# Two joined transformer blocks on one core: other tail of the expert stage, other places for a softplus exponential, weight loads, a copy, a z product, weight differences and a gate tile

## The chip, the cores and the metric

One core of one Trainium2 chip runs the whole program. The metric is the device time of one execution in microseconds (us); all arithmetic is float32. The engines are TensorE (PE, with its weight loads as PEld), VectorE (DVE), ScalarE (ACT), GpSimd (POOL) and SyncE (SP, which here issues most transfers). They run their own instruction lists and wait for each other on semaphores.

## The reference, cut to what matters

The input has 256 tokens of width 1024. The first block is attention over a low-rank key/value, a gated MLP over chunks, and a mixture of 32 experts; the second is two layers, each an RG-LRU branch and an mLSTM branch.

```python
h = rms_norm(x, norm1_g); proj = h @ w_in            # q, ckv, qi, ki, wi, u, v, ga, gb
merged = sigmoid(ga) * (attention @ w_proj_a) + sigmoid(gb) * (gmlp(u, v) @ w_proj_b)
x = x + merged @ w_out
h2 = rms_norm(x, norm2_g)
comb = two experts of one group per token            # router
y = sum over e of comb[:, e] * ((silu(h2 @ w_gate[e]) * (h2 @ w_up[e])) @ w_down[e])
x = rms_norm(x + y, final_norm_g)
for l in range(2):
    shift, scale, gate = split(silu(c) @ w_ada[l] + b_ada[l])
    h = rms_norm(x, norm_g[l]) * (1 + scale) + shift
    rg_x, rg_z, ml_x, ml_o, ml_z = split(h @ w_in[l])
    y_rg = rglru(conv(rg_x), softplus(-lambda)) * silu(rg_z)
    y_ml = norm(sigmoid(ml_o) * mlstm(silu(conv(ml_x)))) * silu(ml_z)
    x = x + gate * (concat(y_rg, y_ml) @ w_out[l])
return rms_norm(x, final_g)
```

## The kernel before, in words

**Weights and slots.** SP issues every big weight as one 1 MB piece (load, L1177 to L1183): 49 first pieces (24 of them slices of w_ada), 96 expert chunks (gate, up, down of 32 experts) and 64 layer pieces. A piece goes to a slot and SP waits until the piece that lay there before is used up. The first and the layer pieces share a ring of 6 slots; the expert chunks use 19 slots, the ring and 13 other buffers that are idle in that stage (L440 to L450). Nine expert chunks are issued between first pieces, behind the pieces of EARLY_LOADS (L87). SP works strictly in order, so a wait for one slot holds all that stand behind it.

**First block.** PE multiplies piece after piece. The order of the first pieces is: two of qi, ada 0, the latent piece, ada 1, two of q, u 0, ada 2, u 1, ada 3, v 0, ada 4, ada 5, v 1, ada 6, ada 7, then gate pieces alternating with ada pieces. An ada piece is not for PE: DVE sums it (ada_sums, L1620), or, for six of them, POOL multiplies it (L2326) and ACT sums the product (ada_job, L1257), ADA_LAG places later than the call asks for. Until that is done its ring slot is taken. After the index scores ACT waits for sp_wanted (L1309), a DVE step (L1659 to L1662), for the exponential of a softplus that only the layers need; behind it on ACT stand the copies of K and V out of PSUM (L1311 to L1314), without which PE has no free bank for V (L588). Then come u, v, two gate jobs (L623) and the loop over 8 heads (L625), in which PE turns the probabilities of head g once DVE has them ready (L635).

**Expert stage.** The router's counts decide an order of the experts; only the six fixed experts (18 chunks) can be asked for before it is known (L1218 to L1221). Nine units (gate_up_own, turn, down_own, gather, mix; L790 to L841) take two or four experts each, every expert in its own 32 or 64 columns of the array. mix(u) adds the result of a unit to the tokens: 4 matmuls on PE, 4 additions on DVE (L1880). After the last unit DVE adds and takes statistics (L1930 to L1948), POOL multiplies by final_norm_g (L2350), ACT squares (L1438), and from both sums come the scales for the first layer's input, written to rdiag (L1962), with which PE turns x (L926).

**Layers.** In each layer PE computes rx, ri, then z, x and o products by a seven-product scheme for 2 x 2 blocks (in_product, L949), which needs differences of weights (in_sums, weight_sums on DVE) and a combination of the products (in_combine on DVE, whose first product is copied by ACT in pair_copy, L1485). Then follow q, k, v, the transposed v (mv, L1032), a gate tile (out_gate_tile, L988), the input and forget gates (gr, L1044 to L1052), more gate tiles, the mz0 products, scores and the output products. From the gates DVE derives rows of decays (L2067 to L2087), then in_combine of mz0, z_mul(0) and weigh(0) (L2132); weigh(h) is what the first PE product of head h (L1093) waits for. z_mul(1) and weight_sums(0, 1) stand behind the norm of the heads (L2156 to L2165), then the products with z (L2170), which free the two banks into which PE transposes (L1120), then row_sums.

## Time and profile before

| what | value |
|---|---|
| median of 3 runs | 964.5 us (962.47 to 965.26) |
| profiled execution, time | 968.08 us |
| its span | 966.4 us |
| granted TensorE clock, mean | 0.965 of full |
| PE busy | 883.1 us, 91% of the span |
| DVE, ACT, POOL busy | 553.7, 252.6, 98.1 us |
| DMA | 229.58 MB, mean 238 GB/s |

The page has the busy time of each engine, a strip of 40 slices, the chain of work that ended last and the costliest groups of instructions. The profiled execution took 1.68 us more than its span and 3.6 us more than the median. Where PE is nearly always busy, time is lost only in its waits and in stretches in which the granted clock is the lower of its two levels (1.2 instead of 2.4 GHz, shown as 0.50 of full speed).

### The profile page before, as it was taken

The page shows a single profiled execution, that of the slowest core. Times are in us where ns is not written, and L with a number is a line of the kernel's source. Part 1 is how long each engine was busy: PE and PEld are TensorE (multiplying, and loading weights), DVE is VectorE, ACT ScalarE, POOL GpSimd, SP SyncE. Part 2 cuts the span into 40 slices and gives each one's busy share as a digit, 9 for nine tenths or more (in the row PEclk, how much of TensorE's full clock was granted, in tenths as well). Part 3 has the DMA queues.
Part 4 walks back from the last instruction along what each step waited for, and adds up shares of the span by engine and source line. Part 5 has one row for each costly group of instructions (what it writes and reads, how often), then busy time and mean ns, then how long its engine had stood idle before and what let it go on. Part 6 is the DMA issues. An engine that isn't in the chain of part 4 may idle for free.

```text
span 966.4 us, 14575 instructions
## 1 busy us (share of the span) xinstructions
PE 883.1 (91%) x5710; PEld 717.1 (74%) x5710; DVE 553.7 (57%) x1086; ACT 252.6 (26%) x546; POOL 98.1 (10%) x104
## 2 busy tenths in 40 slices
PE   7979899999999976777799999998999999999896
PEld 6848687888755633443588988887878898889785
DVE  4276767665421301111566896687746689668793
ACT  2334523102311111110327034122121804412311
POOL 5252300002000000000200000060000000006011
PEclk9989899999999988998899999999999999999999
DMA  9925876599899999999364335222443434522221
GB/s 342 401 83 200 349 322 251 216 408 422 347 423 422 420 420 421 419 422 421 149 160 168 142 145 193 89 87 88 174 174 132 168 131 159 215 91 88 110 87 44
DMA packets 35128, 229.58 MB, mean 238 GB/s; under 512 B 5984, under 2 KB 6016, under 8 KB 8176
## 3 DMA queue, kind: packets, MB, share of 16 engines
q1 hardware_dynamic: 30944, 222.05, 58.0%
q0 software_dynamic: 1312, 4.71, 1.4%
q10 hardware_dynamic: 2800, 1.85, 0.6%
q8 instruction: 47, 0.77, 0.3%
q14 instruction: 25, 0.20, 0.1%
HBM read 227.54 MB, written 1.06 MB: 237 GB/s over the span
## 4 chain that ended last, share of the span: by engine, by line
PE 68%; SPq 10%; DVE 9%; ACT 6%; DMA 4%; issue 3%; POOL 0%; ACTq 0%; DVEq 0%; POOLq 0%
PE bank L495 15%; SPq L1183 9%; PE bank L970 8%; PE bank L1109 8%; PE bank L937 6%; PE bank L801 3%; PE bank L1011 3%; PE bank L702 3%; DMA s<-in_w_down 3%; PE bank L966 3%; PE bank L773 2%; PE bank L816 2%; PE bank L991 2%; PE bank L533 2%; PE bank L487 1%
## 5 line engine op out<-in xcount | busy, mean ns | idle before, releaser
L495 PE MATMUL bank<-hT,ring 128*128 128x256 f32 x512 | 116.6, 386 | 3.7 <-DMA ring<-in_first_pieces 3.4
L495 PEld LDWEIGHTS bank<-hT,ring 128*128 128x128 f32 x512 | 98.2, 194 | 19.1 <-DMA ring<-in_first_pieces 3.8
L1874 DVE SCALAR_TENSOR_TENSOR z<-z,bank 128x256 f32<-128x256 f32 x9 | 3.8, 422 | 150.7 <-ACT z L1405 150.7
L1109 PE MATMUL bank<-ring,s 128*128 128x256 f32 x256 | 61.1, 392 | 1.0 <-issue 1.0
L801 PE MATMUL bank<-s,z 128*32 128x256 f32 (+1 forms) x448 | 44.3, 406 | 16.6 <-DMA ring<-in_w_up 6.0
L1109 PEld LDWEIGHTS bank<-ring,s 128*128 128x128 f32 x256 | 50.3, 198 | 9.0 <-issue 1.7
L801 PE MATMUL bank<-ring,z 128*32 128x256 f32 (+1 forms) x336 | 41.7, 446 | 15.3 <-DMA hT<-in_w_up 6.2
L937 PE MATMUL bank<-hT,ring 128*128 128x256 f32 x256 | 55.6, 379 | 0.0
L937 PEld LDWEIGHTS bank<-hT,ring 128*128 128x128 f32 x256 | 48.5, 190 | 6.5
L2365 POOL TENSOR_TENSOR z<-ring 128x1024 f32<-128x1024 f32 x4 | 9.4, 2353 | 392.5 <-PE bank L970 392.3
L801 PEld LDWEIGHTS bank<-s,z 128*32 128x32 f32 (+1 forms) x448 | 24.7, 119 | 31.1 <-issue 24.0
L801 PEld LDWEIGHTS bank<-ring,z 128*32 128x32 f32 (+1 forms) x336 | 21.8, 133 | 27.4 <-issue 23.3
L970 PE MATMUL bank<-hT,ring 128*128 128x128 f32 x320 | 37.7, 276 | 2.8 <-DVE z L1997 2.8
L970 PEld LDWEIGHTS bank<-hT,ring 128*128 128x128 f32 x320 | 36.7, 192 | 3.8 <-issue 3.7
L970 PE MATMUL bank<-rxp,ring 128*128 128x128 f32 x320 | 39.0, 274 | 0.0
L970 PEld LDWEIGHTS bank<-rxp,ring 128*128 128x128 f32 x320 | 37.5, 192 | 0.1
L773 PE MATMUL bank<-mxp,tmp 128*128 128x128 f32 x288 | 35.6, 284 | 0.2 <-issue 0.2
L773 PEld LDWEIGHTS bank<-mxp,tmp 128*128 128x128 f32 x288 | 34.2, 198 | 0.9 <-issue 0.3
L839 PE MATMUL bank<-z 128*128 128x512 f32 x72 | 33.3, 605 | 0.8 <-ACT z L1418 0.8
L2326 POOL TENSOR_TENSOR ring<-ring,rxp 128x2048 f32<-128x2048 f32 x6 | 27.1, 4520 | 43.1 <-DVE s L1656 23.9
L1405 ACT ACTIVATE z<-bank 128x256 f32<-128x256 f32 x9 | 3.5, 384 | 102.8 <-PE bank L801 102.8
L702 PE MATMUL bank<-ring,z 128*128 128x256 f32 x128 | 28.9, 381 | 1.0 <-DVE z L1729 1.0
(482 smaller groups left out, 1830.0 us busy)
## 6 DMA issues: line engine op xcount, KB each, us to landing
ring<-in_layer_pieces SPq DMA_DIRECT2D x64, 1024.0 KB, 4.8
ring<-in_first_pieces SPq DMA_DIRECT2D x49, 1024.0 KB, 8.0
s<-in_w_gate SPq DMA_DIRECT2D x15, 1024.0 KB, 17.5
s<-in_w_down SPq DMA_DIRECT2D x14, 1024.0 KB, 27.0
s<-in_w_up SPq DMA_DIRECT2D x13, 1024.0 KB, 14.0
ring<-in_w_up SPq DMA_DIRECT2D x11, 1024.0 KB, 20.8
ring<-in_w_gate SPq DMA_DIRECT2D x10, 1024.0 KB, 23.5
ring<-in_w_down SPq DMA_DIRECT2D x9, 1024.0 KB, 23.0
```

Source lines behind the costliest of these rows:

```text
L495: mm = pe.matmul(b[:, 0:T], w[:, (k0 + kb) * CW + m * P:(k0 + kb) * CW + (m + 1) * P], rhs[:, kb, :], start=(kb == 0), stop=(kb == nk - 1))
L702: mm = pe.matmul(b[:, 0:CW], mgT[:, kb, tt * P:(tt + 1) * P], w[:, kb, :], start=(kb == 0), stop=(kb == KB - 1))
L773: mm = pe.matmul(psum[hf][:, kb * P:(kb + 1) * P], xg[:, tt, c:c + P], pick[:, q, tt, :], start=(tt == 0), stop=(tt == TT - 1))
L801: mm = pe.matmul(psum[3][part, c * FF:(c + 1) * FF], hgT[:, kb, part], wt[g][:, kb, :], start=(kb == 0), stop=(kb == KB - 1))
L839: pe.matmul(psum[MIX_BANKS[r]][:, :], combT[:, u % 2, (r // 2) * P:(r // 2 + 1) * P], ye[:, (r % 2) * 512:(r % 2 + 1) * 512], start=True, ...
L937: mm = pe.matmul(b[:, 0:T], w[:, kb * CW + m * P:kb * CW + (m + 1) * P], hT[:, kb, :], start=(kb == 0), stop=(kb == KB - 1))
L966: mm = pe.matmul(half, h_block(r, kb), ws[w][:, kb, :], start=(kb == 0), stop=(kb == 3))
L970: mm = pe.matmul(half[:, m * P:(m + 1) * P], ws[w][:, kb, m * P:(m + 1) * P], h_block(r, kb), start=(kb == 0), stop=(kb == 3))
L1011: mm = pe.matmul(b[:, m * T:(m + 1) * T], w[:, 2 * h + k, m * P:(m + 1) * P], src(2 * h + k), start=(k == 0), stop=(k == 1))
L1109: mm = pe.matmul(product_at(p, i), ys[r][:, kb, :], ws[w][:, kb, :], start=(kh == 0 and kb == 0), stop=(kh == 1 and kb == 3))
L1183: sp.dma_start(slots_of[i][:, :], src).then_inc(slot_full[i], 16)
L2326: step(g.tensor_tensor(w, w, csb.unsqueeze(1).broadcast_to([P, 2, D]), ALU.mult), S["ada_scaled"])
```

## The change

It is made of these parts.

1. ACT waits for sp_wanted and takes the softplus exponential behind the copies of K and V instead of ahead of them.
2. ADA_LAG is 0 instead of 1: ACT sums each POOL product one place earlier; the ninth ada_job, after the second gate copy, goes.
3. EARLY_LOADS is (20, 22, 24, 26, 41, ...) instead of (14, 18, 22, 41, ...): ten early chunks instead of nine, the first of them behind piece 20. A new 8 KB buffer per partition, ws, is a twentieth expert slot; it is paid for by putting tri into rxp, and onesr, sel4 and rdiag into ws (POOL writes onesr and sel4 only after the last unit).
4. In the units mix(u-1) stands between the gate and the up products of unit u instead of behind them, DVE's mix_add(u-1) ahead of act_own(u), and gather(u+1) ahead of turn(u).
5. The very last down chunk is loaded in two halves; PE takes the other three experts of the last unit first, then the first half of the last expert, then the second. The last mix goes in the order 0, 2, 1, 3, and its first two matmuls need only the first half of ye.
6. The norm after the experts: sums of squares of x and of x times final_norm_g instead of statistics; ACT takes five of the eight, DVE three; POOL multiplies three quarters, DVE the fourth.
7. Layers: pair_copy of rz0 stands in the middle of ACT's loop over 8 heads instead of behind it; gate tile (2, 0) stands ahead of mv and tile (2, 1) ahead of gr; z_mul(1) stands ahead of the wait for the squares; the fourth difference of weight_sums(0, 1) stands behind row_sums; in combine an addition to x stands behind the next product.

```diff
+LAST_ORDER = (0, 2, 1, 3)
-ADA_LAG = 1
+ADA_LAG = 0
-EARLY_LOADS = (14, 18, 22, 41, 42, 43, 44, 45, 48)
+EARLY_LOADS = (20, 22, 24, 26, 41, 42, 43, 44, 45, 48)
...
+        ws_t = sb("ws", [P, 2048])
+        sel4 = ws_t[0:MLH, 0:MLH * P].rearrange("p (h t) -> p h t", h=MLH)
+        onesr = ws_t[0:MLH, 512:512 + P]
+        rdiag = ws_t[:, 768:768 + TT * P].rearrange("p (t c) -> p t c", t=TT)
...
-        moe_slots = [RING + i for i in (7, 8, 6, 0, 2, 3, 1, 4, 5, 10)] + [(NB1 + i) % RING for i in range(RING)] + \
-            [RING + i for i in (9, 11, 12)]
+        moe_slots = [RING + i for i in (7, 8, 6, 11, 0, 2, 3, 1, 4, 5, 10)] + [(NB1 + i) % RING for i in range(RING)] + \
+            [RING + i for i in (9, 12, 13)]
...
                 for c, done in ((0, S["gate_done"]), (1, S["gu_done"])):
+                    if c == 1 and u >= 1:
+                        mix(u - 1)
...
+                wt = [loaded(j0 + g, 2)[:, :].rearrange("p (k c) -> p k c", k=2) for g in range(G - 1)]
                 for hf in range(2):
                     for k in range(2):
+                        for g in range(G - 1):
+                            product(g, wt[g], hf, k)
+                pe.wait_ge(S["last_half"], 16)
+                w = slots_of[slot[expert_chunk[j0 + G - 1, 2]]][:, :].rearrange("p (k c) -> p k c", k=2)
+                for hf in range(2):
+                    product(G - 1, w, hf, 0)
+                loaded(j0 + G - 1, 2)
+                for hf in range(2):
+                    product(G - 1, w, hf, 1)
...
-                pe.wait_ge(S["ye_ready"], u * 2 + 2)
+                pe.wait_ge(S["ye_ready"], u * 2 + (2 if u < NU - 1 else 1))
...
+                w = full(chunk())
+                out_gate_tile(2, 0, w)
                 pe.wait_ge(A.free, A.upto(f"vn{l}11"))
...
-                w = full(chunk())
-                out_gate_tile(2, 0, w)
+                out_gate_tile(2, 1, w)
+                used()
                 pe.wait_ge(A.free, A.upto(f"mv{l}3"))
...
-                out_gate_tile(2, 1, w)
-                used()
...
+                if n == E0 + 3 * EXPERTS - 1:
+                    sp.dma_start(slots_of[i][:, 0:1024], src[:, 0:1024]).then_inc(S["last_half"], 16)
+                    sp.dma_start(slots_of[i][:, 1024:2048], src[:, 1024:2048]).then_inc(slot_full[i], 16)
...
-            act.wait_ge(S["sp_wanted"], 1)
-            step(f(labs, labs, ACT.Exp, scale=-1.0), S["sp_ready"])
             for m in range(4):
                 out_copy(kvT[:, m, :], T)
             for tt in range(TT):
                 out_copy(vnat[:, tt, :], 512)
+            act.wait_ge(S["sp_wanted"], 1)
+            step(f(labs, labs, ACT.Exp, scale=-1.0), S["sp_ready"])
...
+            for n in range(3):
+                if n < 2:
+                    act.wait_ge(S["moe_out"], n + 1)
+                    last_square(x, n, 8, 1)
+                act.wait_ge(S["xg_out"], n + 1)
+                last_square(xn, n, 16, n // 2)
             roots(small[:, 2:4])
...
+                for h in range(KB):
+                    if h == KB // 2:
+                        pair_copy("rz0")
...
+            v.wait_ge(S["gfin_loaded"], 16)
+            step(tten(last_part(xn, 3), last_part(x, 3), gfin[:, 512:D], ALU.mult))
+            last_square(x, 2, 8)
+            last_square(x, 3, 8)
+            last_square(xn, 3, 16)
+
+            roots_n["ssq"] += 5
             v.wait_ge(S["ssq_ready"], roots_n["ssq"])
-            step(tten(small[:, 9:10], small[:, 9:10], small[:, 10:11], ALU.add))
-            step(stt(small[:, 2:4], small[:, 8:10], 1.0 / D, small[:, 6:8], ALU.mult, ALU.add), S["root_wanted"])
+            step(tten(ms1, small[:, 8:10], small[:, 10:12], ALU.add))
+            step(tsc(small[:, 6:8], ms1, EPS / D, EPS * EPS, ALU.mult, ALU.add))
+            step(tten(small[:, 16:18], small[:, 16:18], small[:, 18:20], ALU.add))
+            step(stt(small[:, 2:4], small[:, 16:18], 1.0 / D, small[:, 6:8], ALU.mult, ALU.add), S["root_wanted"])
...
+                z_mul(1)
                 roots_n["ssq"] += 8
                 v.wait_ge(S["ssq_ready"], roots_n["ssq"])
...
-                z_mul(1)
-                weight_sums(0, 1)
+                weight_sums(0, 1, (0, 1, 2))
...
                 row_sums()
+                weight_sums(0, 1, (3,))
                 weight_sums(1, 0)
...
-                    add_to_x(4 * p + 1, last)
+                    gate_it(4 * p + 1, last)
                     step(tten(low, product(5), low, ALU.add))
+                    into_x(4 * p + 1, last)
```

## Rows read from the trace of the kernel before

**Rows 1.** PE's waits, 56 to 256 us: engine, line, released by, us, times, longest.

```profile
PE bank L588 <- ACT s L1253: 6.8, 1, 6.8
PE bank L495 <- DMA ring<-in_first_pieces: 3.4, 1, 3.4
PE bank L602 <- DMA ring<-in_first_pieces: 0.8, 1, 0.8
```

**Rows 2.** Stretches: us, us, busy PE PEld DVE ACT POOL, clock, DMA share, GB/s.

```profile
60.00:70.00 10.00, 4.59 (x9) 2.42 (x10) 9.38 (x27) 4.23 (x8) 9.84 (x3) 0.66 0.05 20
...
100.00:110.00 10.00, 8.63 (x28) 7.17 (x29) 8.04 (x10) 6.24 (x10) 4.87 (x2) 0.66 1.01 426
110.00:200.00 90.00, 89.42 (x447) 74.17 (x446) 60.98 (x147) 25.28 (x69) 0.00 (x0) 1.00 0.70 270
200.00:252.00 52.00, 49.39 (x276) 44.23 (x275) 31.43 (x86) 11.69 (x29) 8.79 (x8) 0.97 1.01 421
252.00:257.00 5.00, 5.00 (x91) 3.10 (x93) 1.86 (x9) 0.60 (x1) 0.00 (x0) 1.00 0.37 102
257.00:455.40 198.40, 163.30 (x1540) 95.72 (x1532) 37.29 (x80) 28.40 (x59) 0.61 (x1) 0.93 1.01 420
```

**Rows 3.** First block, in order of time: start us, us, instruction, idle before.

```profile
56.42 2.22 PE L585 MATMUL bank<-s,wg 128*128 128x256 f32 x8
58.72 4.42 DVE L1660 TENSOR_TENSOR lam<-lam,colL 128x16 f32<-128x16 f32 x1
68.98 14.13 PE L495 MATMUL bank<-hT,ring 128*128 128x256 f32 x64
58.61 13.70 POOL L2326 TENSOR_TENSOR ring<-ring,rxp 128x2048 f32<-128x2048 f32 x3 [23.87 <-DVE s L1656]
101.37 9.85 PE L495 MATMUL bank<-hT,ring 128*128 128x256 f32 x32 [3.43 <-DMA ring<-in_first_pieces]
98.53 0.69 DVE L1676 BATCH_NORM_STATS2 s<-s 128x6 f32<-128x512 f32 x1 [9.80 <-ACT s L1253]
115.52 0.35 DVE L1708 TENSOR_SCALAR tmp<-tmp,rt 128x256 f32<-128x256 f32 x1
119.95 0.55 PE L487 MATMUL bank<-ident,tmp 128*128 128x128 f32 x3
```

**Rows 4.** Chain that ended last, around the end of the expert loads: start, us, what.

```profile
427.52 27.91 DMA s<-in_w_down
455.56 3.73 PE bank L816 x32
461.20 0.70 DVE x L1934
464.94 1.28 POOL tmp L2353
470.00 6.41 PE bank L926 x32
```

**Rows 5.** The two z products of layer 0 on DVE.

```profile
637.78 2.97 DVE L2098 SCALAR_TENSOR_TENSOR z<-s,z 128x1024 f32<-128x1024 f32 x1
665.39 1.23 DVE L2098 SCALAR_TENSOR_TENSOR z<-s,z 128x1024 f32<-128x1024 f32 x1
```

**Rows 6.** PE's waits in the layers, 476 to 966 us.

```profile
PE bank L487 <- DVE s L2170: 5.2, 4, 2.2
PE bank L970 <- DVE z L1997: 2.8, 2, 1.4
PE bank L487 <- ACT vaug L1529: 1.5, 2, 0.7
PE bank L1093 <- DVE tmp L2137: 0.8, 1, 0.8
```

**Rows 7.** Gate tile on PE, and DVE after the input gates, layer 0.

```profile
600.29 3.62 PE L991 MATMUL bank<-ring,hT 128*128 128x256 f32 x16
609.72 1.77 DVE L2070 COPY s<-bank 4x256 f32<-4x256 f32 x4 [13.10 <-PE bank L1050]
```

More of the change, by code:

```diff
@@ L1436, in _, with last_square @@
             load_root_table()
-            for n, (tt, lo, hi) in enumerate(((0, 0, D), (1, 0, 512), (1, 512, D))):
-                act.wait_ge(S["xg_out"], n + 2)
-                step(f(squares[:, tt, lo:hi], xn[:, tt, lo:hi], ACT.Square, accum_out=small[:, 8 + n:9 + n]),
-                     S["ssq_ready"])
+            def last_square(src, n, c, half):
+                r = LAST_ORDER[n]
+                cs = slice((r % 2) * 512, (r % 2 + 1) * 512)
+                os = slice(half * 512, (half + 1) * 512)
+                step(f(squares[:, r // 2, os], src[:, r // 2, cs], ACT.Square, accum_out=small[:, c + n:c + n + 1]),
+                     S["ssq_ready"])
+            for n in range(3):
[4 more added lines that the diff above has]
+                last_square(xn, n, 16, n // 2)
             roots(small[:, 2:4])
@@ L1479, in _ @@
                     step(f(thi[:, h, :], b[:, T:2 * T], ACT.Tanh, scale=0.5, bias=hb[:, l, KB + h:KB + h + 1]), A.free)
-                for h in range(KB):
-                    step(f(aa[:, h, :], thr[:, h, :], ACT.Exp, scale=n4[:, 1, h:h + 1], bias=n4[:, 1, h:h + 1]))
-                    step(f(tl[:, h, :], thr[:, h, :], ACT.Tanh, scale=n4[:, 0, h:h + 1], bias=n4[:, 0, h:h + 1]),
-                         S["rg_gate"])
                 def pair_copy(key):
@@ L1491, in pair_copy @@
                     step.skip(A.free, 4)
+                for h in range(KB):
+                    if h == KB // 2:
+                        pair_copy("rz0")
+                    step(f(aa[:, h, :], thr[:, h, :], ACT.Exp, scale=n4[:, 1, h:h + 1], bias=n4[:, 1, h:h + 1]))
+                    step(f(tl[:, h, :], thr[:, h, :], ACT.Tanh, scale=n4[:, 0, h:h + 1], bias=n4[:, 0, h:h + 1]),
+                         S["rg_gate"])
                 if l == 0:
@@ L1530, in _ @@
                                ACT.Copy), A.free)
+                out_copy(oth[:, 0, 2 * CW:3 * CW], CW, ACT.Tanh, scale=0.5)
                 act.wait_ge(S["rg_done"], l + 1)
@@ L1939, in _, with last_add, last_square @@
+            def last_add(n):
+                v.wait_ge(S["mixed"], 4 * NU - 4 + (n + 1))
+                xs = last_part(x, n)
+                step(tten(xs, psum[MIX_BANKS[LAST_ORDER[n]]][:, :], xs, ALU.add), S["moe_out"])
+            def last_square(tensor, n, c):
+                xs = last_part(tensor, n)
+                step(stt(ye[:, 0:512], xs, 1.0, xs, ALU.mult, ALU.mult, accum_out=small[:, c + n:c + n + 1]))
             last_add(0)
-            last_stats(0)
             last_add(1)
-            last_stats(1)
@@ L1943, in _ @@
             last_add(2)
+            v.wait_ge(S["mixed"], 4 * NU)
             last_add(3)
-            last_stats(2)
-            last_stats(3)
-            for tt in range(TT):
-                step(v.bn_aggr(moments[:, 2 * tt:2 * tt + 2], stats[:, 12 * tt:12 * tt + 12]))
-            mean, var = moments[:, 0:4:2], moments[:, 1:4:2]
-            step(tten(ms1, mean, mean, ALU.mult))
-            step(tten(ms1, ms1, var, ALU.add))
-            step(tsc(small[:, 6:8], ms1, EPS, EPS * EPS, ALU.mult, ALU.add))
@@ L1971, in _ @@
                 if l == 0:
-                    step(tsc(small[:, 6:8], ms1, EPS, None, ALU.add), S["root_wanted"])
+                    step(tsc(small[:, 6:8], ms1, 1.0 / D, EPS, ALU.mult, ALU.add), S["root_wanted"])
                     roots_n["n"] += 1
@@ L2292, in _ @@
                                  channel_multiplier=-1))
-            step(g.memset(onesr[:, :], 1.0))
             for _, j0, G in UNITS:
@@ L2349, in _ @@
             g.wait_ge(S["gfin_loaded"], 16)
-            for r in range(4):
+            for n, r in enumerate(LAST_ORDER[0:3]):
                 cs = slice((r % 2) * 512, (r % 2 + 1) * 512)
-                g.wait_ge(S["moe_out"], r + 1)
+                g.wait_ge(S["moe_out"], n + 1)
                 step(g.tensor_tensor(xn[:, r // 2, cs], x[:, r // 2, cs], gfin[:, cs], ALU.mult), S["xg_out"])
+            g.wait_ge(*chunk_free[max(E0 + m for m in range(3 * EXPERTS) if slot[E0 + m] == RING + 11)])
+            g.wait_ge(S["diag_ready"], 2)
+            step(g.memset(onesr[:, :], 1.0))
+            step(g.memset(sel4[:, :, :], 0.0))
+            step(g.affine_select(out=sel4[:, :, :], in_=sel4[:, :, :], compare_op=ALU.not_equal, fill=1.0, base=0,
+                                 pattern=[[-1, MLH], [0, P]], channel_multiplier=1))
             step(g.memset(rxv[:, :, 0:PAD], 0.0))
```

100 lines of the change are left out of this document (48 added, 52 removed).

## The prediction

> **What bounds the kernel now.** I read the strip and the busy times first (PE 91% of the span), then the table of PE's waits, then the stretches, then single instructions. A kernel whose PE is nearly always busy is shortened only where PE waits, where it runs at the lower clock, or where its stretch hangs on the DMA stream. There are three such regions. In the first block PE waits once for ACT (6.8 us) and twice for a weight piece (3.4 and 0.8 us) [rows 1], and behind the two long waits the granted clock of the next 10 us is 0.66, so part of them ran at 1.2 instead of 2.4 GHz [rows 2]. In the expert stage, 257 to 455.4 us, the DMA share is 1.01 at 420 GB/s while PE has idle time: the stream is the bound, it starts when the router's order is known, and 198.4 us later the last chunk lands [rows 2, 4]. From there to the first layer 14.6 us are a chain over all engines [rows 4]. In the layers PE's waits are few and small [rows 6].
>
> **Part 1 and 2, front.** PE is through with K at 58.64 (56.42 and 2.22) and starts u only at 68.98 [rows 3]; between lie the wait of 6.8 us for an ACT copy and the V products at the low clock. The copy stood on ACT behind a DVE step on 16 elements that took 4.42 us beside POOL's multiplication (58.61 on) [rows 3]. With the exponential behind the copies, V can start at 58.7 and takes half of its 3.57 us (68.98 less 65.41, the end of the wait), so u starts at 60.4: 8.6 us. From u's start to the first gate job (68.98 to 101.37) 32.4 us pass, 4.2 of them the two waits for pieces [rows 1, 3]. Both pieces hung on ring slots that ACT frees by ada sums; one place earlier, the first sum comes some 14 us earlier than now (7 by ADA_LAG, the length of one u piece, half of 14.13, and 7 to 8 by PE's own gain), and no early chunk is in front of them. So I take both waits as gone, 12.8 us at the first gate job; whose 9.85 us become 6.9 (half of 14.13 less a little, the same count of columns per matmul at 2.4 GHz): 15.8 us. Now DVE is next: from the last v copy (98.53) to the first finished probabilities (115.87) pass 17.3 us [rows 3], and then PE's transposition, at 119.95 now, waits for them. Last v copy at 89.1, plus 17.3, makes 106.4; some steps that stood behind POOL no longer do, and PE itself comes at 104.3. I take 105.2, between the two: **14.8 us**. Bounds: 15.8 if DVE is never late; 10.3 if DVE's small steps stand behind one more POOL multiplication (13.70 for 3, 4.5 each) [rows 3].
> The heads behind it have 89.4 of 90 us PE busy and a DMA share of 0.70 [rows 2], so a rigid shift passes on to the router. Up to the order's time PE stays the pace: the DMA share in 200 to 252 is 1.01, but it falls to 0.37 in 252 to 257, so the 18 fixed chunks have landed before the order is there [rows 2].
>
> **Part 3, the twentieth slot.** More slots do not raise 420 GB/s, and the chunks that need the order still need it. What is left is the hole of 5 x 0.63 = 3.2 us at 252 to 257 [rows 2]: a second chunk can be asked for with the order at once. Below is 0, above one chunk's time, 1.05 MB at 420 GB/s, 2.5 us; I take **1.2 us**, the middle, having no row nearer. The ring's last expert chunks now are ups and downs of the last unit instead of gates and ups, so SP asks for the first layer pieces later; 198.4 us x 420 GB/s are 83.3 MB against 81.8 MB of 78 chunks, so 1.5 MB of other loads ran in the stream [rows 2]. That they leave it may be worth 0 to 3.6 us; I take 0, since one queue serves in order. The pieces' cover is the tail, 14.6 us for 2.5 us each [rows 4]; were it gone, PE would wait 2.5 us a piece.
>
> **Part 4.** Mix and additions move within units whose PE idles for the stream (163.3 of 198.4 us busy) [rows 2]: 0. Behind PE's new wait stand the up products, for which slots are held longer; see the slower rival.
>
> **Part 5 and 6, tail.** Four experts side by side take 3.73 us for 8 passes, 0.43 each in issue [rows 4]. Three of them can start one chunk (2.5 us) before the last landing, but PE takes its list in order: their eighth pass is issued 3.0 us after their first, so the last expert starts 0.6 us behind the landing and needs 8 passes alone, end at 4.2 us against 3.9 now. The mix needs only the first half of ye, 0.7 us earlier than the second, so the first addition comes 0.4 us earlier. From the first addition to PE are 8.8 us (461.20 to 470.00) [rows 4]. Afterwards DVE has in a row: the last of four additions at 2.6, 0.7 for it, 0.7 for the multiplication, three squares of 0.76, four small steps of 0.2, then root, reciprocal and scaling as now, 1.2: 8.3 us, 0.5 fewer. But DVE's multiplication has both inputs in SBUF and meets POOL's third (1.28 us each, back to back from the first addition on, so until 4.6 or so) [rows 4]; in the trace a DVE step of that kind took 2.97 us beside POOL and 1.23 alone [rows 5]. I add 1.3 us. Tail: 0.4 + 0.5 - 1.3 = **-0.4 us**. Bounds -1.4 and +2.4 (no meeting, and the last expert's products free of the others).
> The Trainium skill speaks against this part: SBUF — State Buffer, Who interferes with whom, says that a VectorE instruction with two SBUF inputs and a GpSimd one that reads SBUF exclude each other for a whole instruction. By that rule the tail is as I take it; without it the median would be 1.3 us lower. The trace's two z products agree.
>
> **Part 7, layers.** (a) rz0's copy comes before PE wants the bank: its wait of 1.4 goes, twice: +2.8 [rows 6]. (b) The gate tile covers the wait for vaug, 0.75 twice: +1.5 [rows 6]. (c) But the input gates now come a tile later, 3.45 - 0.75 = 2.7 us (600.29, 3.62 with its overlap) [rows 7]. DVE works without a gap from its copy at 609.72 to weigh(0), for which PE waits 0.8 us already in layer 0 [rows 6, 7]. Its z product meets POOL in a later part of POOL's work and waits 0.9 us less of the 1.7 [rows 5]. So PE's wait grows by 0.75 + 2.7 - 0.9 = 2.5 us in layer 0 and, with 0.8 us of slack and less given back, 1.8 in layer 1: -4.3. Below: -7; above 0. Late next are scores, heads and norm, all paced by PE. (d) z_mul(1) (1.23 us) [rows 5] fits the gap before the squares arrive, and the fourth difference (as long) leaves the way of L2170: that step starts 2.5 us earlier, held only by the first transposition. Of the 2.6 us per layer that PE waits there [rows 6] I take 1.9: +3.8; bounds 2.4 and 5.2. The fourth difference is wanted four products later and done 5 us ahead of that. (e) The addition put behind a product: 0, DVE waits there for PE. Layers: 2.8 + 1.5 - 4.3 + 3.8 = **3.8 us**.
>
> **Sum.** 14.8 + 1.2 - 0.4 + 3.8 = 19.4 us off the profiled execution's 968.08: 948.7. The median of the runs stands 3.6 us below it: 945.1, so 945.
>
> **Rivals.** *The stream does not move* (A): were the 200 to 252 us at share 1.01 [rows 2] the real pace, the experts' start would gain only the hole (3.2) and the chunk moved ahead (2.5): 5.7 - 0.4 + 3.8 = 9.1, 955.4 us. For it: a share of 1.01. Against: 0.30 of 90 us idle ahead of it [rows 2]. *DVE meets POOL more* (B): front 10.3, 949.6 us. *The gate tile costs nothing* (C): DVE's chain has hidden slack, 940.8 us. *The other side* (D): mix ahead of the up products holds the up slots longer. If each of 8 mixes (about 3.6 us of PE) delays the release by its length and the queue of loads (27.9 us from issue to landing [rows 4]) runs dry, the stream grows by up to 29 us: 974 us. It decides only from 19.4 us of stream idle on; against it stand 35 us of PE idle in the stage. *The extra slot and early chunks do nothing* is within A and the bounds.
>
> **Chances.** Forecast with its bounds 0.65, A 0.12, B 0.10, C 0.08, D 0.05. Range: 937 takes in the upper bounds of front, stream and layers together less what seldom comes together; 956 takes in A. Within 0.3% (2.9 us, what a measurement of this kernel can tell from none) is what lies between D and the rest: 0.02. Faster 0.93, slower 0.05.
>
> **What would show it.** Right: no wait of PE before L588, u at about 60, transposition at about 105, the clock at 1.00 in 60 to 70 and 90 to 100, the order and the last landing 15 to 17 us earlier (439 to 441), waits of L970 and vaug gone, L1093 waiting 2 to 3 us. Wrong: DMA share 1.01 right up to the order (A), a DMA share below 1 in the stage (D), no longer wait before L1093 (C), DVE's multiplication in the tail at 0.7 us.

## The result, and the profile after

| what | before | after |
|---|---|---|
| median of the runs of the first comparison | 964.4 us (962.5 to 965.4, 7 runs) | 959.0 us (956.6 to 960.9, 8 runs) |
| ratio, 95% interval | | 0.9941 (0.9925 to 0.9957) |
| profiled execution, time | 968.08 us | 956.55 us |
| its span | 966.4 us | 954.8 us |
| granted TensorE clock, mean | 0.965 | 0.969 |
| PE, DVE, ACT, POOL busy | 883.1, 553.7, 252.6, 98.1 us | 877.6, 560.3, 252.9, 101.4 us |

The change makes the kernel 5.4 us faster. I forecast 19.4 us, with 937 to 956 as the range; 959 lies outside, on the slow side. An eighth run of the kernel before took 5101.7 us, far from all others, and is in neither the range nor the ratio. On a second chip the same pair stood at 0.9915 (0.989 to 0.994), 9.1 us apart. The two profiled executions are 11.5 us apart because they lie at opposite ends: the one of before 3.6 us above its median, the one of after 2.5 us below. So the traces serve below to place the gains and losses, and the comparisons to size them.

In the first block of the kernel after, in order of time (start, us, instruction), in answer to [rows 3]:

```profile
54.97 2.21 PE L587 MATMUL bank<-s,wg 128*128 128x256 f32 x8
57.02 1.88 PE L590 MATMUL bank<-wg,s 128*128 128x512 f32 x4
58.73 13.98 PE L497 MATMUL bank<-hT,ring 128*128 128x256 f32 x64
...
86.36 7.07 PE L497 MATMUL bank<-hT,ring 128*128 128x256 f32 x32
...
102.64 0.55 PE L489 MATMUL bank<-ident,tmp 128*128 128x128 f32 x3 [0.41 <-DVE tmp L1745]
```

V follows K without a gap, u starts at 58.73 instead of 68.98, the first gate job at 86.36 instead of 101.37 and takes 7.07 instead of 9.85 us, and the first transposition comes at 102.64 instead of 119.95: 17.3 us earlier. PE waits 0.4 us for DVE there. A part of the 17.3 us isn't the change's: already the K products start 1.45 us earlier in this profile (54.97 against 56.42), and in the fifth run below, whose front is that of before, they start at 54.96. From them to the transposition the traces have 63.5 us before and 47.7 after, 15.9 us less.

Around the last expert, PE of the kernel after:

```profile
436.46 5.38 PE L819 MATMUL bank<-ring,z 128*32 128x512 f32 x32 [1.52 <-DMA ring<-in_w_down]
441.77 3.70 PE L865 MATMUL bank<-z 128*128 128x512 f32 x8
451.99 5.49 PE L950 MATMUL bank<-ws,tmp 128*128 128x128 f32 x32 [6.52 <-DVE ws L2004]
```

Against [rows 4] the turn (L950, with which PE turns x for the first layer) starts 18.0 us earlier, so the gain of the front is kept up to there. Now PE's longest wait in the kernel after, and what came of those of [rows 6]:

```profile
PE bank L1105 <- DVE cols L2145: 13.3, 2, 7.0
...
PE bank L489 <- DVE s L2214: 2.2, 4, 0.7
```

The waits before L970 (2.8 us) and for vaug (1.5) are gone, that for the ring of z products has fallen from 5.2 to 2.2. But there is a wait that no row of before has: in each layer PE stands before the second scores (L1105) until DVE has copied the columns of decays out of their bank, 7.0 and 6.3 us. DVE of layer 0 ahead of that copy, and POOL beside it:

```profile
609.65 1.22 DVE L2028 TENSOR_TENSOR s<-ring 128x1024 f32<-128x1024 f32 x1
610.91 3.41 DVE L2028 TENSOR_TENSOR wg<-ring,s 128x1024 f32<-128x1024 f32 x1
614.35 3.25 DVE L2134 TENSOR_SCALAR oth<-oth 128x2048 f32<-128x2048 f32 x1
...
621.14 0.17 DVE L2145 COPY cols<-bank 128x16 f32<-128x16 f32 x1
```

```profile
610.90 2.34 POOL L2411 TENSOR_TENSOR z<-ring 128x1024 f32<-128x1024 f32 x1 [156.50 <-PE bank L994]
613.32 3.20 POOL L2411 TENSOR_TENSOR ring<-ring 128x1024 f32<-128x1024 f32 x1
616.60 3.21 POOL L2411 TENSOR_TENSOR z<-ring 128x1024 f32<-128x1024 f32 x1
619.89 2.36 POOL L2411 TENSOR_TENSOR s<-ring,z 128x1024 f32<-128x1024 f32 x1
```

The same two DVE steps in the kernel before, and POOL's first sum there:

```profile
629.36 1.23 DVE L1986 TENSOR_TENSOR wg<-ring,s 128x1024 f32<-128x1024 f32 x1
630.62 1.23 DVE L2092 TENSOR_SCALAR oth<-oth 128x2048 f32<-128x2048 f32 x1
```

```profile
632.44 2.35 POOL L2365 TENSOR_TENSOR z<-ring 128x1024 f32<-128x1024 f32 x1 [164.33 <-PE bank L970]
```

Before, DVE was through with them at 631.85 and POOL began at 632.44, a margin of 0.6 us. Counted from the start of the q products (576.78 before, 556.20 after), DVE's step on wg now comes 2.1 us later and POOL's first sum 1.0 us earlier, so that the two start within 0.01 us of each other. POOL's 2.34 us pass first, then DVE's step, then POOL's, and so on by turns: DVE pays 3.41 and 3.25 instead of 1.23 each, 4.2 us more, and POOL 3.20 instead of 2.36 in two of its own. In layer 1 it is the same (3.39 and 3.25), 8.4 us in all. Besides, the granted clock is lower in the stretches around the waits (us, us, PE's busy time and count, granted clock, DMA share, GB/s), after:

```profile
620.00:640.00 20.00, 18.63 (x123) 0.85 0.00 1
...
850.00:870.00 20.00, 13.72 (x97) 0.79 0.30 117
870.00:890.00 20.00, 20.00 (x134) 0.87 0.01 1
```

Behind both waits a part of the products runs at 1.2 instead of 2.4 GHz: the scores and z products up to the first head take 7.3 and 7.8 us, and 4.9 at the full clock (twelfth run below). Before, the heads had the full clock in layer 0 and 0.97 in 835 to 895 us.

### The profile page after: what moved, and what is told of

It is laid out like the page before. It is cut to its first block, busy times and chain, and to the rows that moved or that the text cites. A ratio compares the mean times of both kernels' runs of the same rounds, so it can differ in the third digit from the quotient of the medians.

```text
span 954.8 us, 14587 instructions
## 1 busy us (share of the span) xinstructions
PE 877.6 (92%) x5710; PEld 712.9 (75%) x5710; DVE 560.3 (59%) x1086; ACT 252.9 (26%) x550; POOL 101.4 (11%) x103
## 4 chain that ended last, share of the span: by engine, by line
PE 71%; DVE 13%; SPq 9%; DMA 3%; issue 2%; ACT 1%; DVEq 0%; ACTq 0%
PE bank L497 12%; PE bank L994 11%; PE bank L1133 10%; SPq L1211 8%; PE bank L961 6%; PE bank L805 4%; PE bank L1035 3%; PE bank L704 3%; DMA ring<-in_w_down 3%; PE bank L990 3%; PE bank L775 2%; PE bank L819 2%; PE bank L865 2%; PE bank L535 2%; PE bank L1015 1%
## 5 line engine op out<-in xcount | busy, mean ns | idle before, releaser
L497 PE MATMUL bank<-hT,ring 128*128 128x256 f32 x512 | 113.6, 380 | 0.2 <-ACT s L1331 0.2
L1923 DVE TENSOR_TENSOR x<-bank,x 128x512 f32<-128x512 f32 x32 | 22.1, 692 | 113.1 <-issue 82.2
L1133 PE MATMUL bank<-ring,s 128*128 128x256 f32 x256 | 58.3, 380 | 0.9 <-issue 0.9
L961 PE MATMUL bank<-hT,ring 128*128 128x256 f32 x256 | 55.6, 379 | 0.0
L1133 PEld LDWEIGHTS bank<-ring,s 128*128 128x128 f32 x256 | 48.3, 190 | 8.1 <-issue 1.7
L805 PE MATMUL bank<-ring,z 128*32 128x256 f32 (+1 forms) x288 | 34.5, 409 | 7.0 <-DMA ring<-in_w_gate 4.7
L994 PE MATMUL bank<-hT,ring 128*128 128x128 f32 x320 | 40.0, 286 | 0.0
L805 PEld LDWEIGHTS bank<-ring,z 128*32 128x32 f32 (+1 forms) x288 | 18.3, 123 | 17.7 <-issue 11.9
## 6 DMA issues: line engine op xcount, KB each, us to landing
s<-in_w_up SPq DMA_DIRECT2D x16, 1024.0 KB, 17.4
```

The costliest lines, as they stand in the source:

```text
L497: mm = pe.matmul(b[:, 0:T], w[:, (k0 + kb) * CW + m * P:(k0 + kb) * CW + (m + 1) * P], rhs[:, kb, :], start=(kb == 0), stop=(kb == nk - 1))
L805: mm = pe.matmul(psum[3][part, c * FF:(c + 1) * FF], hgT[:, kb, part], wt[g][:, kb, :], start=(kb == 0), stop=(kb == KB - 1))
L961: mm = pe.matmul(b[:, 0:T], w[:, kb * CW + m * P:kb * CW + (m + 1) * P], hT[:, kb, :], start=(kb == 0), stop=(kb == KB - 1))
L994: mm = pe.matmul(half[:, m * P:(m + 1) * P], ws[w][:, kb, m * P:(m + 1) * P], h_block(r, kb), start=(kb == 0), stop=(kb == 3))
L1133: mm = pe.matmul(product_at(p, i), ys[r][:, kb, :], ws[w][:, kb, :], start=(kh == 0 and kb == 0), stop=(kh == 1 and kb == 3))
```

## The experiments

The theory T: the gate tile ahead of the input gates makes DVE late, so late that two more of its steps meet POOL, and the wait that follows costs clock besides. Rivals: R, only the gates' own lateness counts; N, PE makes the time up later. Against these stood the question whether front, stream or tail gave less than I had counted. All comparisons have five rounds; a ratio is to the kernel before on the same chip.

**First: the changed kernel again.**

> The changed kernel once more, unaltered, as the base of the three others and to see how far one profile of it lies from the next. All theories: 0.992 to 0.996 of the kernel before, 956 to 961 us. If the profiled pair's 11.5 us were the change's real worth and the medians' 5.4 us an accident of the runs, it would come out at 0.988 here; if 5.4 is right, the profile of this run should be nearer 959 than 956.5, and PE's waits in it, set beside those of the first profile, should show where 2 to 4 us come and go.

958.2 us (955.7 to 961.2), 0.9915 (0.989 to 0.994). The profiled execution took 961.2 at a mean clock of 0.960, the first one 956.55 at 0.969, and the waits of PE are nearly the same (12.4 instead of 13.3 us ahead of the scores). What comes and goes is the clock: the first transposition lies at 103.68 instead of 102.64, the last down products take 8.29 instead of 5.38 us.

**Second: gate tiles back.** ACT's copies of the two tiles go back with them.

```diff
                 used()
-                w = full(chunk())
-                out_gate_tile(2, 0, w)
                 pe.wait_ge(A.free, A.upto(f"vn{l}11"))
...
-                out_gate_tile(2, 1, w)
-                used()
+                w = full(chunk())
+                out_gate_tile(2, 0, w)
                 pe.wait_ge(A.free, A.upto(f"mv{l}3"))
...
                 mm.then_inc(B.done, 1)
+                out_gate_tile(2, 1, w)
+                used()
                 out_gate(3)
```

> The changed kernel with the two gate tiles of part 7 back in their old places, all else as changed. Theory T (my forecast went wrong because the later input gates put two more DVE steps beside POOL's weight sums): PE's two waits ahead of the scores (7.0 and 6.3 us) shrink to about 1 and 0.5, the wait for vaug (0.75 each) comes back, DVE's fourth difference and the step on the 2048 gate columns fall from 3.4 and 3.3 to 1.23 us each; 13.3 - 1.5 - 1.5 = 10 to 11 us faster than the changed kernel, about 948. Theory R (the gates' own lateness of 2.7 us is all, and the waits have another cause): 3 to 4 us faster, and the waits ahead of the scores stay above 3 us. Theory N (PE gets the time back later): within 2 us of the changed kernel.

943.2 us (942.4 to 943.8), 0.976 (0.9735 to 0.9785): 15.0 us faster than the changed kernel, more than even T said. PE's waits in question:

```profile
PE bank L1117 <- DVE tmp L2181: 1.6, 2, 0.8
PE bank L489 <- ACT vaug L1566: 1.5, 2, 0.7
```

DVE and POOL of layer 0, each by itself again until the z product:

```profile
612.22 1.23 DVE L2028 TENSOR_TENSOR wg<-ring,s 128x1024 f32<-128x1024 f32 x1
613.48 1.23 DVE L2134 TENSOR_SCALAR oth<-oth 128x2048 f32<-128x2048 f32 x1
618.25 0.17 DVE L2145 COPY cols<-bank 128x16 f32<-128x16 f32 x1
620.63 3.33 DVE L2140 SCALAR_TENSOR_TENSOR z<-s,z 128x1024 f32<-128x1024 f32 x1
```

```profile
615.65 2.35 POOL L2411 TENSOR_TENSOR z<-ring 128x1024 f32<-128x1024 f32 x1 [157.72 <-PE bank L994]
```

```profile
620.00:640.00 20.00, 19.22 (x148) 1.00 0.11 46
...
850.00:870.00 20.00, 19.22 (x142) 1.00 0.28 107
870.00:890.00 20.00, 19.51 (x120) 1.00 0.27 105
```

The last three are its stretches: full clock all through. The waits account for 13.3 - 1.6 - 1.5 = 10.2 of the 15.0 us; 4.8 remain. From q's start to the first output product this trace and that of the kernel after differ by 89.86 - 82.31 = 7.5 us in layer 0 and 90.33 - 82.32 = 8.0 in layer 1, so everything lies in that stretch. N falls, and so does R, which gave 3 to 4 us.

**Third: POOL later, the tile left forward.**

```diff
-                g.wait_ge(A.done, A.upto(f"mz0{l}3"))
+                g.wait_ge(B.free, B.upto(f"cols{l}"))
                 w = of_weights(full(slots_of[slot[na]]), full(slots_of[slot[nb]]), extra_of[0])
```

> The changed kernel, in which POOL starts its four weight sums only when DVE has copied the columns of decays, instead of when the mz0 products begin to be finished. Nothing else is altered; the gates stay a tile late. Theory T: DVE's two steps take 1.23 us again, PE's waits ahead of the scores fall by 4.2 us each (to about 2.8 and 2.1), the z product of DVE now meets POOL and takes about 3 us instead of 1.2, which delays the first weighing but not the columns: 6 to 8.5 us faster than the changed kernel. POOL ends its row sums at about 638 instead of 628.6 us, still ahead of the first output product (646). Theory R: the two waits stay at 5 us and more, under 3 us gained. A third, P (the output products then wait for POOL): as slow as the changed kernel or slower, with a new wait of PE for POOL at the output products.

948.2 us (947.0 to 952.1), 0.9825 (0.9798 to 0.9852): 10.1 us gained by the medians, 8.7 by the ratios, without touching PE's order, and more than the 6 to 8.5 that T gave. DVE's step on the gates at 613.17 takes 1.23 us again, and its z product 1.41 instead of the 3 us that I expected; PE's wait and the stretches:

```profile
PE bank L1105 <- DVE cols L2145: 4.4, 2, 2.8
```

```profile
620.00:640.00 20.00, 20.00 (x150) 1.00 0.03 4
...
850.00:870.00 20.00, 18.39 (x98) 0.74 0.29 106
```

So some 60 to 67% of the loss hang on the meeting of DVE and POOL. What remains against the second run, 5.0 us, is the lateness that my forecast priced: 4.4 us of wait less the 3.1 that the second run has, and lower clock in layer 1. From q's start to the first output product it comes to 1.1 us in layer 0 and 4.0 in layer 1. T.

**Twelfth, told here: the wait filled with idle products.** The changed kernel; the products' results are not used.

```diff
                         for k in range(2):
                             mm = pe.matmul(b[:, o:o + T - c * P], mkT[:, 2 * h + k, c * P:(c + 1) * P],
                                            mqT[:, 2 * h + k, c * P:T], start=(k == 0), stop=(k == 1))
+                    for _ in range(28 if h == 0 else 0):
+                        mm = pe.matmul(b[:, T + P:T + 2 * P], mqT[:, 0, 0:P], mqT[:, 0, 0:P], start=True, stop=True)
                     mm.then_inc(B.done, 1)
```

> The changed kernel itself, gate tile forward, with 28 idle matmuls of 128 columns in each layer behind the first scores, where PE waits for DVE's copy of the columns; their results go to unused columns of the bank. They stand wholly inside the wait of 7.0 and 6.3 us, so they save nothing by themselves. If the lower clock behind that wait is a part of the loss (15 us against 10.2 us of waits), PE's wait shrinks to under 1 us each, the granted clock stays 1.00 behind it and the time falls by 3 to 5 us, to 953 to 956. If the loss is the waits alone: within 1 us of the changed kernel, or slower by what the idle products overrun.

954.2 us (952.1 to 954.8), 0.9872 (0.9849 to 0.9896), against 0.9915 for the changed kernel on another chip: 4.1 us, which the two intervals leave open between 1 and 7. The traces agree: from q's start to the first output product 88.2 us in either layer, against 89.9 and 90.3, 3.8 us less. PE of layer 0 and the stretches:

```profile
614.20 2.05 PE L1105 MATMUL bank<-s 128*128 128x256 f32 x8
616.03 7.62 PE L1108 MATMUL bank<-s 128*128 128x128 f32 x56
623.49 1.47 PE L1105 MATMUL bank<-s 128*128 128x256 f32 x8
624.80 3.74 PE L994 MATMUL bank<-hT,ring 128*128 128x128 f32 x32
```

```profile
620.00:640.00 20.00, 20.00 (x159) 1.00 0.00 1
850.00:870.00 20.00, 20.00 (x150) 0.91 0.29 110
870.00:890.00 20.00, 20.00 (x153) 1.00 0.01 1
```

Useless work in the wait makes the kernel faster: the z products behind it take 3.7 us, where the kernel after needed 4.7. The clock falls here too (0.91 in 850 to 870), but it is back before the idle products end, so that only the first scores (2.05 us instead of 1.57 in layer 0) and a part of the idle products run slowly. From the end of the wait to the first product of the first head PE needs 4.9 us in either layer, where the kernel after needed 7.3 and 7.8: 5.3 us is what the clock cost behind the two waits. The idle products overrun the waits (9.3 us instead of 8.6 from the first scores to the second, twice 0.75), and 5.3 - 1.5 is the 3.8 above. It fits the 4.8 that the waits left open.

**Fifth: the gate tiles alone, on the kernel before.** The edit is the second one, the other way about.

> The kernel before with the two gate tiles of part 7 alone moved, nothing else. Theory T (later gates, two DVE steps beside POOL's sums, and the lower clock behind the wait): as in the changed kernel, 7.5 us lost in each layer against the version with the tiles back, so 13 to 16 us slower than the kernel before, PE waiting 6 to 7 us twice ahead of the scores, granted clock below 0.9 in the 20 us behind each. Theory I (the loss needs another part of the change, the rz0 copy or the earlier PE in the layers): 3 to 7 us slower. My forecast's own price for it was 2.8 us net (4.3 lost, 1.5 gained).

981.4 us (975.3 to 984.4) against 965.5, ratio 1.0172 (1.0137 to 1.0208): 16 us slower. PE's wait ahead of the scores is 13.4 us in two, the longest 7.2, and the granted clock is 0.92 and 0.85 in 640 to 660 and 890 to 910 us. The loss needs no other part of the change.

**Fourth and eighth: the front.** Parts 1 and 2 alone, then part 1 alone, on the kernel before.

```diff
-            act.wait_ge(S["sp_wanted"], 1)
-            step(f(labs, labs, ACT.Exp, scale=-1.0), S["sp_ready"])
             for m in range(4):
                 out_copy(kvT[:, m, :], T)
             for tt in range(TT):
                 out_copy(vnat[:, tt, :], 512)
+            act.wait_ge(S["sp_wanted"], 1)
+            step(f(labs, labs, ACT.Exp, scale=-1.0), S["sp_ready"])
```

> The kernel before with parts 1 and 2 alone (exponential behind the copies, ADA_LAG 0, first early chunks behind pieces 20, 22, 24 instead of 14, 18, 22; still nine early chunks and 19 slots). If the front passes on to the end as the two traces have it (17.3 us at the router, 1.5 of them ahead of the first difference in code), it is 14 to 16 us faster than the kernel before: 949 to 951, ratio 0.984 to 0.985, and the rest of the change loses about 10. If the kernel's real gain at the front is smaller than the pair of profiles shows, for instance because the kernel before usually does better than in its profile, it is 6 to 10 us faster. If the stream does not move: under 5 us.

> The kernel before with part 1 alone (the exponential behind the copies of K and V). My working gave the u products 8.6 us earlier by it and the rest of the front's 14.8 us to the two waits for pieces and the clock behind them. If part 1 is worth what it gives at u: 7 to 9 us faster, 958 to 960 on this chip, and both waits for pieces still there. If the two waits for pieces grow by what PE gains, since their slots are freed by ACT's sums at the old time: 0 to 4 us faster. If they vanish too because ACT itself comes earlier: 13 to 16 us faster, and ADA_LAG and the early chunks are worth nothing.

Parts 1 and 2: 947.7 us, 0.9809 (0.9781 to 0.9836), against 967.3: 19 us, by the interval 16 to 21, and more than the 14 to 16 that I expected. In its trace the first transposition comes at 104.89, 15.1 us earlier than before (15.9 counted from the K products), and the last down products 15.7. The two profiled spans lie 17.9 us apart; 1.8 of them come behind the first output product of layer 1 (62.8 and 61.1 us to the end), where no code differs. Part 1 alone: 957.8 us, 0.9926 (0.9898 to 0.9954), 7 us; u starts at 59.89, 9.1 us earlier, but both waits for pieces are still there:

```profile
PE bank L495 <- DMA ring<-in_first_pieces: 3.6, 1, 3.6
...
PE bank L602 <- DMA ring<-in_first_pieces: 0.8, 1, 0.8
```

Its first transposition is at 109.72, 10.2 us earlier. So part 2 takes the two waits and brings a further 5 us in the traces (5.9 counted from the K products). The comparisons put it at 11 us, with 7 to 15 as the interval; the two profiled runs lie at opposite ends, 2.5 us above the median of the fourth and 3.0 below that of the eighth, which is most of the gap.

**Sixth: the last down chunk in one load**, gate tiles back.

```diff
-                if n == E0 + 3 * EXPERTS - 1:
-                    sp.dma_start(slots_of[i][:, 0:1024], src[:, 0:1024]).then_inc(S["last_half"], 16)
-                    sp.dma_start(slots_of[i][:, 1024:2048], src[:, 1024:2048]).then_inc(slot_full[i], 16)
-                else:
-                    sp.dma_start(slots_of[i][:, :], src).then_inc(slot_full[i], 16)
+                sp.dma_start(slots_of[i][:, :], src).then_inc(slot_full[i], 16)
```

> The changed kernel with the gate tiles back (as in the second run) and, besides, without part 5: the last down chunk is one load, and the four experts of the last unit are multiplied side by side again. The comparison is with the second run, 943.2 us. Theory S (a lone expert's eight passes behind the others cost more than the early start gives, above all where the granted clock is the lower): the down products of the last unit, 5.4 to 8.3 us from start to end of the group in the profiles so far, become 3.7 to 4.4 and start 0 to 1 us later; 1 to 4 us faster. Theory F (my forecast's term): within 0.5 us. The other way (the landing in halves did bring something): 0.5 to 1.5 us slower.

944.4 us, 0.9792 (0.9769 to 0.9816), against 0.976 (0.9735 to 0.9785) with the split: not faster, rather 1 to 3 us slower; my theory S falls. Its PE:

```profile
439.74 5.42 PE L819 MATMUL bank<-ring,z 128*32 128x512 f32 x32 [4.16 <-DMA ring<-in_w_down]
445.09 3.70 PE L850 MATMUL bank<-z 128*128 128x512 f32 x8
```

In the second run the down products start at 437.61 and take 7.76 us, and the mix comes at 445.30, though its front was 1.3 us later (105.06 against 103.73). So the split brings 1.1 us by these two traces. Counted in the same way, the seven other traces with the split and the new order of the mix lie between 0.4 us worse and 3.6 better than the sixth, the best where the down products have the full clock; in the sixth itself they ran partly at the lower one (5.42 instead of 3.73 us). The sixth also shows when the last chunk landed: 15.8 us earlier than before, while the front was 16.2 us earlier. In the fourth run, which hasn't the twentieth slot, the two are 15.7 and 15.1. So no trace shows a gain by the slot; it wasn't run alone.

**Seventh and ninth: POOL behind the first z product**, gate tiles back.

```diff
-                g.wait_ge(A.done, A.upto(f"mz0{l}3"))
+                g.wait_ge(S["zm_ready"], 2 * l + 1)
```

> The changed kernel with the gate tiles back, and POOL's four weight sums held until DVE has done the first z product. DVE's z product met POOL in the second run (3.3 instead of 1.2 us) and PE waited 0.8 us in each layer for the weighing behind it. Theory T: z product at 1.23 us, PE's wait for the weighing gone: 1.5 us faster than the second run, 941.7; POOL would end its row sums about 5 us ahead of the first output product. If POOL becomes late: a new wait of PE for POOL at the output products, 0 to 5 us slower.

> The seventh run's kernel once more (changed kernel, gate tiles back, POOL's sums behind the first z product), as the base on the same chip for the next two. Ratio to the kernel before 0.973 to 0.978, 940 to 942 us.

939.9 us, 0.9754 (0.9729 to 0.9779), and 941.0, 0.9745 (0.9724 to 0.9766). In the seventh run's trace DVE's z product takes 1.23 us, and POOL's sums, now undisturbed, 2.35 to 2.37 each:

```profile
620.28 2.37 POOL L2411 TENSOR_TENSOR z<-ring 128x1024 f32<-128x1024 f32 x1 [163.84 <-DVE z L2140]
622.72 2.35 POOL L2411 TENSOR_TENSOR ring<-ring 128x1024 f32<-128x1024 f32 x1
```

PE's wait of 0.8 us for the first weighing is gone in both layers, and the stretch from q to the first output product is 81.26 us against 82.31: 2.1 us in all by the traces, too little for the comparison with the second run to settle. With the tenth, which can't be told from it, this is the fastest version that I ran, and it beats both kernels: 25 us below the kernel before on its chip, and, by the ratios (0.9745 and 0.9915), 16 below the changed one.

**Tenth: the norm as before.** Statistics on DVE, four multiplications on POOL, three squares on ACT, last mix in the order 0, 1, 2, 3; all else as in the ninth.

```diff
-LAST_ORDER = (0, 2, 1, 3)
+LAST_ORDER = (0, 1, 2, 3)
...
             last_add(0)
+            last_stats(0)
             last_add(1)
+            last_stats(1)
             last_add(2)
-            v.wait_ge(S["mixed"], 4 * NU)
             last_add(3)
-            v.wait_ge(S["gfin_loaded"], 16)
-            step(tten(last_part(xn, 3), last_part(x, 3), gfin[:, 512:D], ALU.mult))
-            last_square(x, 2, 8)
-            last_square(x, 3, 8)
-            last_square(xn, 3, 16)
+            last_stats(2)
+            last_stats(3)
```

> The base without part 6 and without the last mix's new order: statistics and scales as in the kernel before, additions 0, 1, 2, 3, POOL multiplies all four quarters. My forecast gave parts 5 and 6 together -0.4 us, of which +0.4 for the earlier first addition, +0.5 for the shorter chain and -1.3 for DVE's multiplication beside POOL. Profiles so far: last mix to the turn 10.2 us with part 6, 10.0 without. So within 1 us of the base by both; if the meeting of DVE and POOL is what eats it, this run's chain from the first addition to PE is 8.8 us and the base's 9 or more, although it has less to do.

941.1 us, 0.9741 (0.9722 to 0.9761): no difference. From the first addition to the end of the scales' writing it needs 8.8 us (445.22 to 454.05), the ninth run 9.2 (445.57 to 454.73). DVE in the ninth run:

```profile
448.90 0.69 DVE L1989 TENSOR_TENSOR tmp<-x,wg 128x512 f32<-128x512 f32 x1
449.63 1.64 DVE L1981 SCALAR_TENSOR_TENSOR z<-x 128x512 f32<-128x512 f32 x1
...
451.31 0.69 DVE L1981 SCALAR_TENSOR_TENSOR z<-x 128x512 f32<-128x512 f32 x1
```

The meeting with POOL is there, but it strikes the first square (1.64 instead of 0.69) and not the multiplication. The statistics of the tenth run, one input on SBUF, pass beside POOL unhindered (0.69 at 447.40, POOL at work from 447.51).

**Eleventh: the mix behind the up products again**, all else as in the ninth (the additions on DVE, gather and its copies too).

```diff
-                    if c == 1 and u >= 1:
-                        mix(u - 1)
...
+                    else:
+                        mix(u - 1)
+                        turn(u)
+                        if u + 1 < NU:
+                            gather(u + 1)
```

> The base without part 4: mix(u-1) behind the up products, its additions behind DVE's product of gate and up, gather(u+1) behind turn(u). My forecast: no difference (rival D: the new order dries the stream, this run up to 29 us faster). In the profiles, those with the new order have the lower clock at the last down products in four of six and those with the old one in none of four; if that belongs to the order of the mix, this run is 1 to 3 us faster than the base; if it belongs to chance or to the twentieth slot, within 1 us.

942.6 us, 0.9756 (0.9738 to 0.9774): not faster, 1.6 us slower by the medians, with intervals that overlap. Part 4 does no harm; rival D is out. The lower clock at the last down products goes with the new order all the same: six of nine profiles with it have it (the group with the split takes 7.0 to 8.3 us there, 5.4 at the full clock), none of five with the old. Only this run of the five has the other parts of the change, so the order of the mix as the cause is likely and not shown. It brings no gain to be rid of it, since with the old order the last down products start later (442.54 against 436.25). Why three of nine escape is open.

## Why the prediction was wrong

The forecast erred by 14 us, and one term has nearly all of it. In the forecast's order:

| step | forecast | measured |
|---|---|---|
| parts 1, 2: first transposition | 14.8 | 15.8 to 16.0 counted from the K products in all traces with both but the eleventh (14.9) |
| part 3, twentieth slot | 1.2 | no gain seen (last landing 15.8 with the front 16.2 earlier) |
| parts 5 and 6, tail | -0.4 | +1.1 for the split (-0.4 to +3.6), 0 for the norm |
| 7, rz0's copy | +2.8 | +3.3 (z to q, 65.3 to 63.7 us, twice) |
| 7, z product and fourth difference | +3.8 | +3.4 (1.9 and 1.5) |
| 7, gate tile | -2.8 net | -15.0 |
| sum | 19.4 | 5.4 and 9.1 in two comparisons; the rows add up to 8.7 |

**The front** was right in mechanism and 1 us too small: V and u came as worked out, both waits for pieces went, and DVE is only 0.4 us late behind them. (The forecast's own sum has a slip that changes nothing: 119.95 less 15.8 is 104.15, where it has 104.3.) Counted from the start of the trace the gain is 14.8 to 17.4 us. That spread lies ahead of the K products, and goes with the clock of the start: in 10 to 20 us it was 1.00, 0.83 and 0.66 in three profiles of nearly the same code, which reach K at 54.97, 55.92 and 57.28. By the fourth run's comparison parts 1 and 2 alone are worth 16 to 21 us, which is more than I forecast. All parts but these and the gate tiles then are worth 4.7 us on the same chip (0.976 against 0.9809, 1 to 8 by the intervals), where the rows of the table give 7.8.

**The stream** gave what the front gave it and no more. For the step "a second chunk can be asked for with the order at once" no trace shows anything.

**The layers' gains** came as worked out. One thing the forecast left out in them: behind the waits for the ring of z products the next 24 products ran partly at the lower clock before (6.41 and 7.03 us, 5.34 after), 2.8 us more in this pair of profiles; in the fourth run, with the same waits, it was 6.02 and 5.35.

**The gate tile** is the step that failed, and within it two sentences. "DVE works without a gap from its copy at 609.72 to weigh(0)" was right, and I took its lateness of 2.7 us through to PE, with 0.9 given back where the z product met POOL. I looked only at the meeting that the trace already had, not at what would be moved into a new one. POOL's start hangs on PE's mz0 products, which come *earlier* with the change, while DVE's chain hangs on the input gates, which come *later*; the margin between them was 0.6 us in the trace of before, and 3.1 us were taken off it. With [rows 5] (2.97 against 1.23) in hand, each further step that meets POOL was to be priced at 1.7 us or more; with the 4.2 us a layer that the two steps turned out to cost, the term of -4.3 would have become -12.7, beyond my lower bound of -7. The second omission is the clock: I counted what a wait gives back where one goes, in the front, but not what it takes where a new one comes. The traces of the twelfth run give that as 5.3 us, and with the 10.2 us of waits it makes up the 15.5 by which the second run's stretches are shorter. The forecast also looked for the wait at the first product of a head; it came a step earlier, at the scores, whose bank hangs on the copy of the columns.

With -15.0 in place of -2.8 the same working gives 945.1 + 12.2 = 957.3, against 959.0 measured. None of the rivals was right: B had DVE meet POOL more often, but in the front, where PE waits 0.4 us for it; C had the gate tile cost nothing; A (the stream stays) gave a time near the measured one for a wrong reason, since the experts' start and the last landing did move by what the front gained.

## What to carry to other kernels

When a change delays one engine's chain, list every instruction of it that shares something with another engine's instructions near in time, and measure the margin between them in the trace: a delay larger than the margin costs not only itself but the rest of the other engine's instruction at each step (2.0 to 2.2 us here, of POOL's 2.35). Ask also what starts the other engine: here the same edit brought it forward. And a new wait on TensorE is to be priced with the slower products behind it; if it cannot be removed, moving the *other* engine's work (one changed wait on POOL, 9 to 10 of 15 us) may be cheaper than moving PE's.

## What was not expected of the hardware

The meeting of VectorE and GpSimd goes by turns and costs both: two DVE steps 3.41 and 3.25 instead of 1.23, two POOL steps 3.20 instead of 2.36, in one stretch of 9 us. The scalar addition on 2048 columns (L2134), with a single tensor input in SBUF, was held just like the differences with two. The Trainium skill has a rule for this (SBUF — State Buffer, Who interferes with whom): `tensor_scalar` is among the operations that can run in a mode that takes the pair of ports shared with GpSimd, and then each blocks the other. The trace agrees, with 3.25 against 1.23 us.

Idle matmuls inside a wait made the kernel some 4 us faster. The clock's fall, though, doesn't need a wait. Layer 1 of the third run in short stretches, around PE's wait of 1.6 us (from 858.25 to 859.87):

```profile
854.00:855.00 1.00, 1.00 (x4) 1.00 0.99 123
856.00:858.00 2.00, 2.00 (x8) 0.50 0.98 414
858.00:860.00 2.00, 0.39 (x3) 0.50 1.03 438
860.00:865.00 5.00, 5.00 (x20) 0.50 0.00 0
```

And the same place in layer 1 of the kernel before, where PE doesn't wait:

```profile
879.00:881.00 2.00, 2.00 (x9) 0.50 0.99 418
882.00:884.00 2.00, 2.00 (x19) 1.00 0.35 147
```

In both the clock is down while PE works without a gap, behind the small transpositions and products from four rows that spread the decays (L1094, L1070 before). Before, it is back within 4 us, without a wait; in the third run it stays down over the wait and 6 us of work behind it. In layer 0 of the kernel after the wait came first: PE stood from 614.4 on, and the clock fell at about 619.4. So a wait can bring the lower clock or lengthen it. Whether those products have a part in the fall isn't shown, nor why layer 0 of the third run and both layers of the second kept 1.00. The clock is also the main difference between the two profiled executions of the kernel after (956.6 and 961.2 us): of their 4.7 us, 0.95 lie ahead of the K products, 2.9 in the last down products and 0.5 in the turn.
